# Layer 0's experts by streamed tables and dense products instead of gathered rows

## The reference, cut to what matters

```python
PEER_HEADS, PEER_TOPK, PEER_NKEYS = 8, 16, 128      # 16384 experts = 128 x 128
def peer_ffn(h, wq, k1, k2, u, v):                  # h: 256 tokens x 1024
    q = (t @ wq).reshape(n_tok, PEER_HEADS, 2, PEER_HALF)
    v1, i1 = lax.top_k(einsum(q[:, :, 0], k1), 16)
    v2, i2 = lax.top_k(einsum(q[:, :, 1], k2), 16)
    sc, pos = lax.top_k(v1[..., :, None] + v2[..., None, :], 16)
    idx = i1 * 128 + i2  (taken at pos)             # 8 heads x 16 = 128 experts a token
    gate = softmax(sc)
    act = gate * gelu(sum_d t[n, d] * u[idx[n, k], d])
    y[n] = sum_k act[n, k] * v[idx[n, k]]
```

## Time and profile before

| what | us |
|---|---|
| median of 3 runs | 1924.44 |
| lowest and highest | 1923.53, 1927.61 |
| the profiled execution's own time | 1927.03 |
| its span, first to last instruction | 1925.2 |
| granted TensorE clock, mean | 0.874 of full |

### The profile page before, as it was taken

How to read it: one execution, slowest core, us unless ns; L and a number is a source line. 1 busy time by engine, 2 the same in 40 slices (tenths; PEclk the granted TensorE clock), 3 DMA queues, 4 the chain that set the end, 5 groups by cost and what they waited for, 6 DMA issues and landing times.

```text
span 1925.2 us, 22276 instructions
## 1 busy us (share of the span) xinstructions
PE 1529.6 (79%) x7828; PEld 912.6 (47%) x7828; DVE 1334.0 (69%) x3962; ACT 418.5 (22%) x1139; POOL 583.4 (30%) x551
## 2 busy tenths in 40 slices
PE   6999999965656889888889687998889875555555
PEld 6644876511113656666558265766656641111111
DVE  6667646769976779585446776877845579778654
ACT  1221211000002722622211264154121210000001
POOL 0110223444442322322222322232232244444541
PEclk8999798667678989999899898999998987886887
DMA  9988499999998967987999998699699999999995
GB/s 368 360 319 308 183 402 376 411 422 421 421 421 356 421 270 273 421 317 277 393 409 417 391 398 321 223 388 373 232 385 396 421 379 403 421 421 421 422 422 227
DMA packets 100255, 703.32 MB, mean 365 GB/s; under 512 B 15264, under 2 KB 15648, under 8 KB 16560
## 3 DMA queue, kind: packets, MB, share of 16 engines
q0 software_dynamic: 78336, 570.46, 73.6%
q1 hardware_dynamic: 21808, 131.45, 17.0%
HBM read 700.82 MB, written 1.05 MB: 365 GB/s over the span
## 4 chain that ended last, share of the span: by engine, by line
PE 43%; DMA 20%; DVE 15%; issue 5%; ACT 5%; POOL 1%; SPq 0%; DVEq 0%; POOLq 0%; ACTq 0%
PE PS L1646 15%; DMA vb<-in_peer_uv,idx 8%; DMA ub<-in_peer_uv,idx 6%; PE PS L1796 3%; PE PS L1702 3%; PE PS L2013 3%; PE PS L1989 3%; DMA ring<-in_peer_uv,idx 2%; DVE vb L1147 2%; PE PS L1970 2%; DVE ub L1147 2%; PE PS L1749 2%; PE PS L1873 1%; ACT ring L1472 1%; DMA mods<-in_peer_uv,idx 1%
## 5 line engine op out<-in xcount | busy, mean ns | idle before, releaser
L1646 PE MATMUL PS<-ub,z 128*64 128x512 f32 x832 | 342.7, 762 | 128.4 <-DVE z L1113 125.0
L1646 PE MATMUL PS<-vb,z 128*64 128x512 f32 x828 | 318.4, 748 | 106.9 <-DVE z L1113 105.2
L2046 POOL DMA_INDIRECT ub<-in_peer_uv,idx x208 | 227.4, 1093 | 522.4 <-PE PS L1646 458.2
L2046 POOL DMA_INDIRECT vb<-in_peer_uv,idx x207 | 230.8, 1115 | 434.9 <-PE PS L1646 389.2
L1359 ACT ACTIVATE tanhs<-cubed 128x2 f32<-128x2 f32 x256 | 52.0, 203 | 879.0 <-DVE cubed L1102 855.5
L1646 PEld LDWEIGHTS PS<-ub,z 128*64 128x64 f32 x832 | 77.8, 162 | 279.0 <-DVE z L1113 184.4
L1646 PEld LDWEIGHTS PS<-vb,z 128*64 128x64 f32 x828 | 73.7, 160 | 262.9 <-DVE z L1113 170.4
L1147 DVE CUSTOM_DVE_ANT_0 vb<-vb,h 128x1024 f32<-128x1024 f32 x104 | 127.1, 1222 | 54.0 <-DMA vb<-in_peer_uv,idx 53.4
L1646 PE MATMUL PS<-mods,z 128*64 128x512 f32 x204 | 124.8, 743 | 36.9 <-DVE z L1113 34.5
L1147 DVE CUSTOM_DVE_ANT_0 ub<-ub,h 128x1024 f32<-128x1024 f32 x104 | 127.1, 1222 | 35.7 <-DMA ub<-in_peer_uv,idx 33.6
L1106 DVE SCALAR_TENSOR_TENSOR acts<-tanhs,gated_x 128x2 f32<-128x2 f32 x256 | 40.4, 158 | 152.4 <-ACT tanhs L1359 146.1
(11 more groups left out here) (364 smaller groups left out, 2780.2 us busy)
## 6 DMA issues: line engine op xcount, KB each, us to landing
ring<-in_gdn_qkv SPq DMA_DIRECT2D x32, 1024.0 KB
ring<-in_peer_wq SPq DMA_DIRECT2D x23, 1024.0 KB
two_slots<-in_ada_wide POOLq DMA_DIRECT2D x20, 1024.0 KB, 7.8
ring<-in_gdn_z SPq DMA_DIRECT2D x16, 1024.0 KB
ring<-in_gdn_w_out SPq DMA_DIRECT2D x16, 1024.0 KB
ring<-in_gla_w_in SPq DMA_DIRECT2D x6, 2048.0 KB, 11.0
mods<-in_ada_wide POOLq DMA_DIRECT2D x11, 1024.0 KB, 7.5
ring<-in_ada_w SPq DMA_DIRECT2D x4, 2048.0 KB, 11.9
```

The source lines that it names most:

```text
L1646: last = pe.matmul(y[64 * g:64 * g + 64, e, :], z[:, i % 4, g, :], rows[:, D + e * 512:D + (e + 1) * 512], start=False, stop=False, skip_g ...
L2046: pool.indirect_dma_start(row_buffers[b], None, uv_rows, off).then_inc(row_landed[b].sem, 16)
```

## The change

Layer 0's two gather stretches are replaced by one dense stage over all 256 tokens and all 16384 experts. Layer 1's experts keep the gathers.

- **Tables.** `peer_ut` and `peer_vt` are layer 0's u (transposed) and v in 64 blocks each of 256 experts, 1 MB a block. SP loads them one after another into three slots `stream` (`table_load`).
- **u phase.** For each of 64 blocks PE does 16 products of 256 columns: all tokens against 256 experts. ACT takes the gelu of the 128x512 result, and issues a DMA that writes it to a buffer in HBM (`spill`).
- **Gates.** Routing stays, but leaves the chosen first and second index and the gate in `picks`. PE transposes these, and for each token DVE makes a one-hot of the first index times the gate and POOL a one-hot of the second index. PE multiplies the two (4 tokens in a step, 64 steps), which gives the token's gate for every expert; ACT copies it into `store`, 128 KB a partition, 2 x 128 x 128 values. The former buffers `mods`, `vb`, `ring`, `two_slots` and `ub` become parts of `store`.
- **v phase.** For each of 64 blocks the activations come back from HBM (DMA issued by ACT, six buffers), DVE multiplies them into `store`, and PE does 8 products of 512 columns into four PSUM banks.
- **Order.** Both tiles' residual follows at the end of the v phase, and only then layer 1's mixer for tile 0. Stretch 2 is planned to begin where mixer 0 ends. `W_AT` and `S2_AT` change: layer 1's mixer of tile 0 had due time 386 and has 544, its tile 1 had 906 and has 1024.

The diff's core (waits and unpacking left out at "..."):

```diff
-            A, B = 382.0, 520.0
-            W_AT = (0.0, A, A + B, A + 2 * B, 2 * A + 2 * B)
+            def pair_at(i):
+                return 30.0 + 4.2 * i
+            def tokens_at(q):
+                return 80.0 + 3.4 * q if q < NB // 2 else 196.0 + 3.0 * (q - NB // 2)
+            def taken_at(j):
+                return 302.0 + 3.7 * j
+            S2_AT = (544.0, 1024.0)
+            W_AT = {2: 1020.0, 3: 1540.0, 4: 1922.0}
...
+                    def table_load(n):
+                        if n >= 3:
+                            sp.wait_ge(table_used.sem, n - 2)
+                        src = peer_ut[n] if n < NB else peer_vt[TAKEN[n - NB]]
+                        sp.dma_start(stream[:, n % 3, :], src).then_inc(landed[n % 3].sem, 16)
...
 (vector)
+                            for e in range(4):
+                                last = dve.tensor_scalar(hots[:, q % 2, 0, e, :], across[:], by_slot[:, t, 0, j + e:j + e + 1], by_slot[:, t, 2, j + e:j + e + 1], ALU.is_equal, ALU.mult)
...
+                            both = store[:, :, 2 * i:2 * i + 2, :].rearrange("p t i n -> p t (i n)")
+                            dve.tensor_tensor(both, both, acts_.rearrange("p (t m) -> p t m", t=T), ALU.mult).then_inc(weighted.sem, 1)
 (scalar)
+                                act.activation(acts_of[4 + i % 2]..., PS[:, i % 2, :]..., ACT.Gelu_apprx_tanh).then_inc(acted.sem, 1)
+                                if i < NB - 2:
+                                    act.wait_ge(acted.sem, i + 1)
+                                    act.dma_start(spill[i], acts_of[4 + i % 2]).then_inc(spilled[i % 2].sem, 16)
...
+                                act.activation(store[:, t, :, j:j + 4], PS[:, 3 + i % 2, :].rearrange("p (n i) -> p i n", n=4), ACT.Copy).then_inc(stored.sem, 1)
 (tensor)
+                                for b in range(2):
+                                    for k in range(KD):
+                                        last = pe.matmul(PS[:, i % 2, b * S:(b + 1) * S], w[:, b, k, :], hT[:, k, :], start=(k == 0), stop=(k == KD - 1))
...
+                                for e in range(4):
+                                    last = pe.matmul(PS[:, 3 + i % 2, e * P:(e + 1) * P], hots[:, i % 2, 1, e, :], hots[:, i % 2, 0, e, :], start=True, stop=True)
...
+                            for b in range(2):
+                                for t in range(T):
+                                    for e in range(2):
+                                        last = pe.matmul(PS[:, SUMS[t][e], :], store[:, t, 2 * i + b, :], rows[:, b, e * 512:(e + 1) * 512], ...)
 (gpsimd)
+                            for e in range(4):
+                                last = pool.tensor_scalar(hots[:, q % 2, 1, e, :], across[:], by_slot[:, t, 1, j + e:j + e + 1], None, ALU.is_equal)
```

More of the change, by code:

```diff
@@ L123, in trunk_kernel @@
         rr = sb(ctx, "rr", [P, 16])
-        landed = [signal(f"weights_landed{i}") for i in range(RING)]
+        landed = [signal(f"blocks_landed{i}") for i in range(RING)]
         used = signal("weights_used")
@@ L177, in trunk_kernel @@
         row_landed = [signal(f"rows_landed{i}") for i in range(11)]
+        back = [signal(f"activations_read{i}") for i in range(6)]
         def blocks_of(w):
@@ L192, in trunk_kernel @@
         sources = {"first": ada, "in": gla_in, "out": blocks_of(gla_w_out)}
-        stream = [sources[kind][b] for kind, b in PLAN]
-        slot_of, turn_of_slot = [i % RING for i in range(len(stream))], [i // RING + 1 for i in range(len(stream))]
+        stream_blocks = [sources[kind][b] for kind, b in PLAN]
+        slot_of, turn_of_slot = [i % RING for i in range(len(stream_blocks))], [i // RING + 1 for i in range(len(stream_blocks))]
         def block_at(i):
@@ L463, in _ @@
                     sp.dma_start(gng[:], gla_norm_g[0].partition_broadcast(P)).then_inc(small.sem, 16)
-                    for i in range(RING, len(stream)):
+                    for i in range(RING, len(stream_blocks)):
                         load_block(sp, i)
@@ L829, in decoder @@
             zero = sb(scr, "zero", [P, P])
-            z = sb(scr, "z", [P, 4, 2, P // 2])
+            z = stream[:, 2, D:D + 4 * P].rearrange("p (i g n) -> p i g n", i=4, g=2)
+            sc0 = extra.rearrange("p (c n) -> p c n", n=NK)
+            picks = sb(scr, "picks", [P, T, 3, P])
+            across = sb(scr, "across", [P, P])
+            h_flat = h[:].rearrange("p t d -> p (t d)")
+            by_slot = h_flat[:, D:D + 2 * 3 * P].rearrange("p (t a n) -> p t a n", t=T, a=3)
+            acts_of = [hots[:, i // 2, i % 2].rearrange("p e n -> p (e n)") for i in range(4)] + [h_flat[:, 0:512], h_flat[:, 512:1024]]
+            NB = NK // 2
+            spill = nc.dram_tensor("spill", [NB, P, 4 * P], F32, kind="Internal").ap()
+            TAKEN = [NB - 2, NB - 1] + list(range(NB - 2))
+            SUMS = ((3, 4), (5, 6))
             cand = sb(scr, "cand", [P, 2, K2])
@@ L1344, in experts @@
                         exp(0)
-                        for w in range(4):
+                        for k in range(1, 2 * PAIRS):
+                            yield 5.0 + 18.0 * (k - 1) + 13
+                            exp(k)
+                        yield ROUTE_AT[2] + 14
+                        exp(2 * PAIRS)
+                        for w in (2, 3):
                             exps = [(dot_at(w, SP_ * p + first + 10), j) for p in range(PAIRS) for j, first in routed_in(w, p)]
@@ L1608, in scores_out @@
                         for t in tiles:
-                            last = act.activation(sc[:, t * C + 2 * b:t * C + 2 * b + 2, :], PS[:, 5 + i % 2, 256 * t:256 * t + 256].rearrange("p (c n) -> p c n", n=NK), ACT.Copy)
+                            last = act.activation(sc0[:, t * C + 2 * b:t * C + 2 * b + 2, :], PS[:, 5 + i % 2, 256 * t:256 * t + 256].rearrange("p (c n) -> p c n", n=NK), ACT.Copy)
                         last.then_inc(sc_ready.sem, 1)
-                    interleave(experts(), mixer())
+                    interleave(experts(), dense(), mixer())
                 @block.tensor
```

265 lines of the change are left out of this document (191 added, 74 removed).

## The result

The changed kernel takes 2455.5 us, median of three runs (2443.6 to 2456.2), where the kernel before takes 1924.4. The ratio is 1.274, 95% interval 1.267 to 1.280: 27% slower. The forecast was 2472, range 2405 to 2570.

The account below looks back on a forecast made before the run. PE's own products were taken to bound the dense stage, with transfers and other engines hidden. 278.7 + 995 + 3 + 362 + 3 + 498.6 + 332.5 = 2472.8 us of span, so 2472 us, 28% slower, range 2405 to 2570.

Parts of the forecast that it names:

- Up to the first u product: Before the dense stage: 14.8 us of expert products, sums' opening and a layout step leave PE's order, 293.5 to 278.7.
- The dense stage: u phase, v phase, one-hots and mod blocks on PE: 978.8 us, plus 8 for clock and 8 for waits, 995.
- Why nothing else sets the pace: Dense stage: DMA, ACT, DVE and POOL work per block fits beside PE's 7 to 8 us, so PE is busy nearly throughout.
- Mixer 0 alone: Layer 1's mixer for tile 0, without gathers beside it: 456 us falls by 94 to 362.
- two convolutions: In mixer 0: ACT's 8.2 us replaces 13.84 between pairs of input blocks; eight of these save 45 us.
- two cores: In mixer 0: a level falls from 7.99 to 6.1 us; ten levels and about as many outside pairs save 29 us.
- gate, output, query blocks: In mixer 0: 24 blocks; the gate's eight fall from 37 to 31 us, the three groups together save 20 us.
- Layer 1's stretches: Layer 1's expert stretches after mixer 0: 3 us for late first gathers, then old lengths 498.6 and 332.5 with tail.
- A: Rival: the dense stage is bound by its transfers, 416 us, and the kernel is faster, about 1893 us; chance 1%.
- B: Rival: products cost less in a long stream, u and v blocks half, 444 us less, time 2028 us; chance 2%.
- C: Rival: PE waits in the dense stage on ACT's queue, POOL's one-hots or read-back; 1 us a block gives 2600; 13%.
- D: Rival: mixer 0 is no faster alone and takes 456 us, time 2566 us; chance 4%.

## Why the prediction was right

**What bounds the kernel.** The reading of the earlier trace rows held: gathers alone are DMA bound, gathers beside a mixer nearly free. The removed overlap costs 186 us by itself, which the prediction had only implicitly, in its pieces.

**Up to the first u product.** Forecast 278.7, measured 285.5. The step is right all the same. The output product, ahead of all that changed, starts at 179.31 where it was 172.29; from there to the first u product are 106.1 us, and the forecast had 278.7 - 172.3 = 106.4. Other runs whose code is the same up to here start the u phase at 278.3 to 284.7. So this one came late by run-to-run variation, and its 7 us cover a part of the misses below.

**The dense stage.** Forecast 995, measured 982.4. By terms: u blocks 64 x 6.91 = 442 (forecast 448.0: the 7.00 a block ran to the start of an expert pair, 0.09 more than a block's own 6.91); v phase with the gate row 441.3 (439.7 and 1.8); one-hots 64 x 0.89 = 57 (57.1); `mod` blocks 8 x 3.63 = 29 (29.8). The clock loss was put at 8 between 0 and 15, and the run with few mod products shows 11. The 8 us for waits were 0. The waits (-8.0), the clock (+3), the u blocks (-5.8) and the `mod` blocks (-0.8) are all but 1 of the 12.6 us that the stage came out shorter.

**Why nothing else sets the pace.** Three runs show it: half the u products give back just their own time (219 us where 512 products at 0.432 are 221), the spill gives 2 us and POOL's second helping of one-hots nothing. POOL's one-hot costs 0.63 us, in the lower half of 0.23 to 1.9. The gelu takes 0.59 and the scattered copy 0.60, the bottom of 0.6 to 1.2.

**Mixer 0 alone.** Forecast 362 between 334 and 456, measured 348.8. The mechanism was right: part of the time that the expert pairs had taken from PE comes back. How much in which part was wrong in all three terms, and the errors partly cancel. These rows start the parts before the change (convolution, core, convolution, core; the gate blocks start at 902.43 and the mixer ends at 1059.0):

```profile
615.52 3.82 PE L1796 MATMUL PS<-hT,ring 128*128 128x128 f32 x32
670.03 1.16 PE L1823 MATMUL PS<-tri,g 128*128 128x128 f32 x8
759.23 3.84 PE L1796 MATMUL PS<-hT,ring 128*128 128x128 f32 x32
813.95 1.16 PE L1823 MATMUL PS<-tri,g 128*128 128x128 f32 x8
```

And these after it, with two levels of the first core and the gate blocks (end at 1619.6):

```profile
1282.40 9.02 PE L1957 MATMUL PS<-hT,store 128*128 128x128 f32 x64
...
1311.16 3.57 PE L1940 MATMUL PS<-ones,store 128*128 128x1 f32 x16 [5.01 <-ACT store L1616]
...
1326.64 1.06 PE L1984 MATMUL PS<-tri,g 128*128 128x128 f32 x8
...
1353.17 2.10 PE L2034 MATMUL PS<-store 128*128 128x128 f32 x16
...
1358.99 2.10 PE L2034 MATMUL PS<-store 128*128 128x128 f32 x16
...
1395.20 21.89 PE L1957 MATMUL PS<-hT,store 128*128 128x128 f32 x192 [1.26 <-issue]
...
1432.76 1.06 PE L1984 MATMUL PS<-tri,g 128*128 128x128 f32 x8
...
1501.27 27.86 PE L2131 MATMUL PS<-store,hT 128*128 128x256 f32 x128 [1.26 <-issue]
```

| part | before | after | gained | forecast |
|---|---|---|---|---|
| two convolutions | 109.2 | 81.8 | 27.4 | 45 |
| two cores | 177.7 | 137.1 | 40.6 | 29 |
| gate, output, query blocks | 156.6 | 118.3 | 38.3 | 20 |

The opening ahead of the first convolution gained 1.2 more.

- The convolutions gained less. ACT's chain is 8.3 us a pair (its first copies of the first two pairs start at 1291.57 and 1299.86), just the 8.2 of the forecast; PE makes three pairs in 21.89 in the second convolution, 7.3 each. It runs ahead in the first one too, and then waits 5.01 for ACT (1311.16). But eight times 8.2 are 66 us and the two convolutions take 82. Their beginnings, and the one-column and other steps between the third and the fourth pair, were not in the term.
- The cores gained more. A level is 5.82 us where 6.1 was forecast, but most of it is a slip in the sum: ten levels at 1.9 us and as many pairs outside at 1.94 are 38, not 29.
- The last three groups gained nearly twice the forecast. It looked at the eight gate blocks alone (37 to 31 us; they take 27.9), while expert pairs also stood between and behind the groups.

There is a simpler rule that these rows bear out. Products of the expert pairs kept PE busy for 33.5, 46.4 and 39.9 us in the three parts, and leaving them out gave back 27.4, 40.6 and 38.3, nine tenths in sum. Two of the three misses, 18 us each and of opposite sign, are larger than the 13 us by which the mixer as a whole came out short.

**Layer 1's stretches.** 504.3, where the forecast had 3 for the late first gathers and 498.6, and 330.5 (332.5). All misses together: +6.8 - 12.6 - 13.2 + 2.7 - 2.0 = -18.3, and the span is 18.4 under the forecast of 2472.8. So the total is closer than its parts: the mechanism of the dense stage was right term by term, that of mixer 0 only as a whole.

**The rivals.** A needed a stage under 446 us; it was 982, and 486 with a quarter of the products. B needed half the price for a product in a long stream: 472 v products in a row, and 1024 u products with their breaks, cost what sixteen did. C's waits do not show. D had mixer 0 unchanged; it became 107 us shorter. But B stood close to a truth that I gave away in half a sentence, the number format. The row at 172.29 has two records for each product, and so had every row from which the price came. In 16 bits there is one record, and the price is a quarter. The Trainium skill gives a reason in "FP8 and Floating Point Precision", section "TensorE Precision Notes": true FP32 makes four passes through the array. The trace agrees: 0.432 and 0.109 us for 256 columns, 0.859 and 0.217 for 512. Of "TensorE: Matmul & The Clock Gate", section "Back-to-back issue gap", the runs bear out the formula for an isolated product (N/2.4 + 2.5 ns, so 216 ns for 512 columns and 109 for 256) in 16 bits, back to back. They don't bear out the 131 ns for a stream of 512 columns, which the prediction had weighed: 217 was measured.

## What to carry to other kernels

Before gathered work is turned into dense work, set its products' time at their measured price against the transfer time that it saves: here 982 us of float32 products stood against 650 us of gathers, and no arrangement of the helpers could mend that. Look then at the records of a product: here two for each product went with float32, and a product in 16 bits cost a quarter, which took this change from 27% slower to 3% faster where rounding to 16 bits is acceptable. And price the overlap that a change removes as a term of its own; here it was 186 us, a third of the loss, measured with one run of the old kernel in serial order. A total that comes out right can hide terms that do not: compare it with the trace part by part.

## What the runs showed of the hardware

- A float32 product costs four times a 16-bit one of the same shape (0.432 to 0.109 us at 256 columns, 0.859 to 0.217 at 512, all at full granted clock), and is recorded twice.
- A casting load, float32 in device memory and 16 bits in the core's memory, keeps the rate by the bytes that it reads: 1 MB each 2.76 us, beside read-backs of activations, at a DMA share of 1.05. POOL needs 0.53 to 0.57 us to issue one.
- The same comparison of 128x128 elements takes POOL 0.63 to 0.64 us and DVE 0.31 (both with 16-bit output). The narrower output gains nothing where both were measured: POOL had 0.63 in float32 too, and DVE's compare and multiply went from 0.364 to 0.383.
- Streams of one-column products cost more than themselves: eight of 3.6 us cost 29 us and another 11 in the products behind them, at the lower clock (0.61 granted from 384.5 to 388.9 us behind one of them; 1.00 over the whole u phase with 2 of 16 products in each).
